# Scoring both softmax maps of a differential pair in one pass A unit, and one exponential for both maps in pass B

## What is computed

```python
def diff_block(qp, q):
    s = jnp.einsum('bqhmd,bkhmd->bhmqk', q.astype(f32), kd) * SCALE
    bias = table[t5_bucket(kpos[None, :] - qp[:, None])]
    s = s + jnp.transpose(bias, (2, 0, 1))[None, :, None]
    mask = (kpos[None, :] // CHUNK) <= (qp[:, None] // CHUNK)
    s = jnp.where(mask, s, NEG_INF)
    p = jax.nn.softmax(s, axis=-1)
    a = p[:, :, 0] - lam * p[:, :, 1]
    return jnp.einsum('bhqk,bkhe->bqhe', a, vd)
```

## Time and profile before

| | before |
|---|---|
| median of 3 runs | 2607.59 us (2605.26 to 2613.81) |
| the profiled execution | 2605.0 us |
| its span | 2603.2 us |
| PE busy | 2478.4 us (95%), 13569 instructions |
| DVE busy | 1374.3 us (53%), 2227 instructions |
| ACT busy | 942.9 us (36%), 1869 instructions |
| POOL busy | 386.0 us (15%), 398 instructions |
| granted TensorE clock, mean | 0.984 |

### The profile page before, as it was taken

One profiled execution on the slowest core, in us unless ns is written; L12 is line 12 of the kernel. 1 busy time (PEld: TensorE's weight loads), 2 busy tenths in 40 slices (PEclk: granted clock), 3 DMA queues, 4 the chain that ended last, 5 costly groups with the idle time before them and its releaser, 6 DMA issues.

```text
span 2603.2 us, 35097 instructions
## 1 busy us (share of the span) xinstructions
PE 2478.4 (95%) x13569; PEld 1977.2 (76%) x13569; DVE 1374.3 (53%) x2227; ACT 942.9 (36%) x1869; POOL 386.0 (15%) x398
## 2 busy tenths in 40 slices
PE   7999999999999999999988899899899989999998
PEld 5788888789999999999855565565565556888897
DVE  5311123315443333542368888788788786655553
ACT  4123331112222222111136645654664666322221
POOL 0100001121100000112352113103212242000000
PEclk9999999999999999999989999999999999999999
DMA  5688888958987666888560523235054023544432
GB/s 153 161 223 207 202 210 206 209 138 243 244 237 226 207 215 181 233 206 175 145 158 9 126 50 89 55 77 130 5 131 107 28 83 108 181 133 130 143 118 89
DMA packets 583892, 388.65 MB, mean 149 GB/s; under 512 B 318672, under 2 KB 538776, under 8 KB 577416
## 3 DMA queue, kind: packets, MB, share of 16 engines
q1 hardware_dynamic: 574592, 367.80, 53.8%
q0 software_dynamic: 9136, 18.63, 2.1%
HBM read 284.83 MB, written 134.79 MB: 161 GB/s over the span
## 4 chain that ended last, share of the span: by engine, by line
PE 75%; DVE 6%; SPq 5%; ACT 5%; issue 4%; DMA 3%; POOL 1%; DVEq 0%; ACTq 0%; POOLq 0%
PE p_acc L876 13%; PE p_acc L881 12%; PE p_acc L880 12%; PE a_op L2111 5%; PE a_sb L2086 4%; PE a_sb L2087 3%; PE a_op L2108 3%; PE a_sa L2064 2%; PE a_sa L2067 2%; PE e_U L1428 2%; PE e_U L1430 2%; PE e_U L1429 2%; ACT a_e L1924 2%; DVE a_nmax L1955 2%; PE a_sa L2065 2%
## 5 line engine op out<-in xcount | busy, mean ns | idle before, releaser
L876 PE MATMUL p_acc<-p_h_hi,p_w_hi 128*128 128x384 f32 (+1 forms) x1960 | 716.1, 365 | 11.9 <-DVE p_ev L586 5.5
L881 PE MATMUL p_acc<-p_h_hi,p_w_lo 128*128 128x384 f32 (+1 forms) x1920 | 688.0, 358 | 0.0
L880 PE MATMUL p_acc<-p_h_lo,p_w_hi 128*128 128x384 f32 (+1 forms) x1920 | 687.8, 358 | 0.0
L1955 DVE TENSOR_REDUCE a_nmax<-a_sa 128x1 f32<-128x1024 f32 (+7 forms) x384 | 347.2, 911 | 125.0 <-PE a_sa L2069 45.1
L1924 ACT ACTIVATE a_e<-a_sb 128x512 f32<-128x512 f32 (+3 forms) x640 | 310.4, 533 | 278.5 <-PE a_sb L2087 183.8
L876 PEld LDWEIGHTS p_acc<-p_h_hi,p_w_hi 128*128 128x128 f32 x1960 | 370.8, 189 | 52.7 <-issue 12.8
L881 PEld LDWEIGHTS p_acc<-p_h_hi,p_w_lo 128*128 128x128 f32 x1920 | 362.1, 189 | 30.4
L880 PEld LDWEIGHTS p_acc<-p_h_lo,p_w_hi 128*128 128x128 f32 x1920 | 362.6, 189 | 29.0
L692 DVE TENSOR_TENSOR p_w_lo<-p_raw,p_w_hi 128x1024 fp32r<-128x1024 f32 x96 | 125.6, 1308 | 368.8 <-ACT p_w_hi L619 368.7
L2086 PE MATMUL a_sb<-a_q,a_k 128*128 128x512 f32 (+2 forms) x640 | 276.5, 436 | 20.6 <-ACT a_e L1924 18.1
L2087 PE MATMUL a_sb<-a_q,a_k 68*128 68x512 f32 (+2 forms) x640 | 237.1, 374 | 0.0
(11 more groups left out here) (233 smaller groups left out, 3475.6 us busy)
## 6 DMA issues: line engine op xcount, KB each, us to landing
p_raw<-in_w_in SPq DMA_DIRECT2D x98, 512.0 KB, 5.7
s_k_raw<-scratch_kS SPq DMA_DIRECT2D x64, 512.0 KB, 6.9
scratch_kS<-in_cache_fox_k SPq DMA_DIRECT2D x32, 512.0 KB, 6.6
scratch_kS<-in_cache_diff_k SPq DMA_DIRECT2D x32, 512.0 KB, 6.4
s_v_raw<-in_cache_fox_v SPq DMA_DIRECT2D x8, 2048.0 KB, 11.0
s_v_raw<-in_cache_diff_v SPq DMA_DIRECT2D x8, 2048.0 KB, 10.0
a_q<-scratch_q_hi SPq DMA_DIRECT2D x32, 512.0 KB, 13.3
a_k<-scratch_k_hi SPq DMA_DIRECT2D x32, 512.0 KB, 15.2
```

The source lines that it names most:

```text
L876: nc.tensor.matmul(acc[a % 2][:, 0:n], hi, h_hi[p][:, k, at:at + n], start=(k == 0), stop=False)
L880: nc.tensor.matmul(acc[a % 2][:, 0:n], hi, h_lo[p][:, k, at:at + n], start=False, stop=False)
L881: last = nc.tensor.matmul(acc[a % 2][:, 0:n], lo, h_hi[p][:, k, at:at + n], start=False, stop=(k == DK - 1))
L1955: nc.vector.tensor_reduce(nmax[:, b % 2, c, col:col + 1], scores_of(ev[1]), axes, ALU.max, negate=True).then_inc(a_maxed, 1)
```

## The change

1. Pass A of a differential pair has units of both maps, `(b, None, t, c)`, with chunks of 512 keys. Map m takes bank m of the PSUM tile. PE does the two 128-row products, one per map, and then the two high-times-high products with 64 rows each, map 0 in array rows 0 to 63 and map 1 in rows 64 to 127. For this, `q2` and `k2` of map 1 hold their values in partitions 64 to 127 and the constants in the rows below. There are 160 such units instead of 192.
2. DVE adds one band for both maps (L1952 before) and takes both maxima in one instruction (L1955 before). ACT still makes one exponential per map, since each has its own bias; each now has up to 512 columns.
3. In pass B the two banks are one tile `sb`. One band addition (76 instead of 152 instructions) and one exponential (320 instead of 640) serve both maps. `b_scored` and `e_made` count units, not maps, so PE waits for the whole exponential of unit u before it writes either map of unit u+1.
4. `nmax`, `total` and `gap` hold up to 4 chunks, and the few small instructions that combine chunks do so for all of them at once.

```diff
-        sb_ = [s.ps(f"sb{m}", [P, QUERIES]) for m in range(MAPS)]
+        sb_ = s.ps("sb", [P, MAPS, QUERIES])
...
         for t in range(4):
+            if b // BLOCKS % 2:
+                A_UNITS += [(b, None, t, c) for c in range(Q + 1)]
+                continue
...
+    chunk = lambda b: CHUNK_KEYS // 2 if is_diff(b) else CHUNK_KEYS
+    a_cols = lambda a: a_width(a) * (2 if is_diff(a[0]) else 1)
...
-    a_work = list(itertools.accumulate([0] + [a_width(unit) + STEP for unit in A_UNITS]))
+    a_work = list(itertools.accumulate([0] + [a_cols(unit) + STEP for unit in A_UNITS]))
...
+    def maps_of(a):
+        return sa[a % 2][:].rearrange("p (m n) -> p m n", m=MAPS)
...
             elif ev[0] == "X" and is_diff(A_UNITS[ev[1]][0]):
...
-                nc.scalar.activation(scores_of(ev[1]), scores_of(ev[1]), ACT.Exp, bias=nmax[:, b % 2, c, col:col + 1],
-                                     accum_out=total[:, b % 2, c, col:col + 1]).then_inc(a_summed, 1)
+                for m in range(MAPS):
+                    col, own = 4 * m + t, maps_of(ev[1])[:, m, 0:a_width(A_UNITS[ev[1]])]
+                    last = nc.scalar.activation(own, own, ACT.Exp, bias=nmax[:, b % 2, c, col:col + 1],
+                                                accum_out=total[:, b % 2, c, col:col + 1])
+                last.then_inc(a_summed, 1)
...
             elif ev[0] == "E":
...
-                    nc.scalar.activation(e[:, u % E_SLOTS, m, cols], sb_[m][:, cols], ACT.Exp).then_inc(e_made, 1)
+                nc.scalar.activation(e[:, u % E_SLOTS, :, cols], sb_[:, :, cols], ACT.Exp).then_inc(e_made, 1)
...
-                for m in range(MAPS):
-                    dve.wait_ge(b_scored, 2 * u + m + 1)
-                    nc.vector.tensor_tensor(sb_[m][:, lo:hi], sb_[m][:, lo:hi], band[:, 1, lo - t0 * P:hi - t0 * P],
-                                            ALU.add).then_inc(b_biased, 1)
+                dve.wait_ge(b_scored, u + 1)
+                bias = band[:, 1:2, lo - t0 * P:hi - t0 * P].to_broadcast([P, MAPS, hi - lo])
+                nc.vector.tensor_tensor(sb_[:, :, lo:hi], sb_[:, :, lo:hi], bias, ALU.add).then_inc(b_biased, 1)
...
         def scores_a(a):
+            if is_diff(b):
+                wide = max(a_width(A_UNITS[a]), 2 * P)
+                ks = slice(c * chunk(b), c * chunk(b) + wide)
+                for m in range(MAPS):
+                    nc.tensor.matmul(maps_of(a)[:, m, 0:wide], q1[z][m][:, qs], k1[z][m][:, ks], start=True, stop=False)
+                for m in range(MAPS):
+                    rows = slice(m * HD, m * HD + HD)
+                    last = nc.tensor.matmul(maps_of(a)[:, m, 0:wide], q2[z][m][rows, qs], k2[z][m][rows, ks], start=False, stop=True)
+                last.then_inc(a_scored, 1)
+                return
...
         def scores_b(u):
+            if u:
+                pe.wait_ge(e_made, u)
             for m in range(MAPS):
-                if u:
-                    pe.wait_ge(e_made, 2 * u + m - 1)
```

More of the change, by code:

```diff
@@ L1576, in banded @@
         tile = 4 * (b % BLOCKS) + t
-        first = max((tile - 1) * P, c * CHUNK_KEYS)
-        end = c * CHUNK_KEYS + a_width(a)
+        first = max((tile - 1) * P, c * chunk(b))
+        end = c * chunk(b) + a_width(a)
         return (end - first, first - (tile - 1) * P) if is_diff(b) and first < end else None
@@ L1748, in load_map @@
             rows = slice(m * HD, (m + 1) * HD)
+            high = lo if z and m else hi
             tensor, part, x = ((q1, hi, "q_hi"), (k1, hi, "k_lo"), (q1, lo, "q_lo"), (k1, lo, "k_hi"),
-                               (q2, hi, "q_hi"), (k2, hi, "k_hi"))[n]
+                               (q2, high, "q_hi"), (k2, high, "k_hi"))[n]
             sp.dma_start(tensor[z][m][part, :].bitcast(F32), d[x][pair_of(f), rows, :]).then_inc(maps_in[z][m], 16)
@@ L1896, in scalar @@
                     act.wait_ge(f_dve, dve_at[b, "gap"])
-                    nc.scalar.activation(gap[:], gap[:], ACT.Exp).then_inc(f_act, 1)
+                    now = gap[:, 0:n_chunks(b), :]
+                    nc.scalar.activation(now, now, ACT.Exp).then_inc(f_act, 1)
                 elif ev[2] == 1:
@@ L2041, in scores_a @@
             if (b % BLOCKS, t, c) == (0, 0, 0):
-                pe.wait_ge(maps_in[z][m], 96 * (f // 2 + 1))
-                if m == 0:
+                for m_ in range(MAPS) if is_diff(b) else [m]:
+                    pe.wait_ge(maps_in[z][m_], 96 * (f // 2 + 1))
+                if not m:
                     pe.wait_ge(side_in[z], side_total(f))
@@ L2059, in scores_a @@
                     at = kt * P - k0
-                    if not is_diff(b) and kt == tile and 0 <= at < n_b:
+                    if kt == tile and 0 <= at < n_b:
                         adds.append((slice(at, at + P), causal[:, 0]))
                 high = (q2[z][m][0:ROW_C, qs], k2[z][m][0:ROW_C, k0:k0 + wide])
-                if is_diff(b):
-                    nc.tensor.matmul(out, q1[z][m][:, qs], k1[z][m][:, k0:k0 + wide], start=True, stop=False)
-                    last = nc.tensor.matmul(out, *high, start=False, stop=True)
-                else:
-                    last = nc.tensor.matmul(out, *high, start=True, stop=not adds)
-                    for cols, msk in adds:
-                        last = nc.tensor.matmul(out[:, cols], ident16[:], msk, start=False, stop=True)
+                last = nc.tensor.matmul(out, *high, start=True, stop=not adds)
+                for cols, msk in adds:
+                    last = nc.tensor.matmul(out[:, cols], ident16[:], msk, start=False, stop=True)
             last.then_inc(a_scored, 1)
@@ L2080, in scores_b @@
             ks = slice(kt * P, (kt + 1) * P)
+            if u:
+                pe.wait_ge(e_made, u)
             for m in range(MAPS):
-                if u:
-                    pe.wait_ge(e_made, 2 * u + m - 1)
-                out = sb_[m][:, c0:QUERIES]
+                out = sb_[:, m, c0:QUERIES]
                 qs = slice(Q * QUERIES + c0, (Q + 1) * QUERIES)
                 nc.tensor.matmul(out, k1[z][m][:, ks], q1[z][m][:, qs], start=True, stop=False)
-                nc.tensor.matmul(out, k2[z][m][0:ROW_C + 2, ks], q2[z][m][0:ROW_C + 2, qs], start=False,
-                                 stop=True).then_inc(b_scored, 1)
+                rows = slice(0, P if z and m else ROW_C + 2)
+                last = nc.tensor.matmul(out, k2[z][m][rows, ks], q2[z][m][rows, qs], start=False, stop=True)
+            last.then_inc(b_scored, 1)
         def product(u):
```

88 lines of the change are left out of this document (49 added, 39 removed).

## The result

| | before | changed |
|---|---|---|
| median | 2609.5 us (4 runs, 2605.3 to 2613.8) | 2692.2 us (4 runs, 2691.2 to 2700.9) |
| ratio, 95% interval | | 1.0324 [1.0306, 1.0343] |
| profiled execution, span | 2605.0, 2603.2 us | 2691.9, 2690.2 us |
| attention, first to last product of pass B | 882.4 us | 966.9 us |
| granted clock, mean of the span | 0.984 | 0.979 |

The account below looks back on a forecast made before the run. PE, busy 95% of the span, and what PE waits for were taken as the bound. Terms 21.6 - 18 + 73 = +77 us on the profiled 2605.0 gave 2682, as median 2684; range 2620 to 2735.

Parts of the forecast that it names:

- Pass B's one exponential: Pass B: PE waits for the merged exponential before the next unit; 83 us lost, 73 us after the deduction.
- The need of 1.39 us: Pass B, full unit without band: time from the end of its columns until PE may begin the next unit, 0.46 before.
- The walk: Pass B: waits added over all 319 intervals between units, need against PE's work between; 93.4 us against 10.2 before.
- four groups with fox pass A or none: Pass B intervals, fox beside fox and differential without differential pass A: waits 22.8, 7.8, 14.3 and 23.5 us.
- four places with nothing between: Pass B: 4 intervals where PE has no work between two units; 5.5 us of waits.
- "10 us" taken off: Pass B: deduction from the 83 us, for new waits that only replace PE's waits for DVE.
- The columns and the switch: Pass A: paired row halves save 30.9 us of columns; entering and leaving 64 rows loses 52.5 us.
- pass A's PE time grows by 21.6 us: Pass A: net of columns saved and switches to 64 rows and back, counted whole as 21.6 us lost.
- Pass A's waits: Pass A: fewer PE stalls for ACT's exponential, with longer exponentials counted against it; 18 us gained.
- 1.1 us times 28 intervals: Pass A: intervals with two units fall from 44 to 16, each saving a stall of about 1.1 us.
- the free switch with hidden waits: Rival: 64-row switch costs nothing and pass B's waits hide; 2583 us, deciding under 0.19 us a unit; chance 0.08.
- ACT: Rival: ACT becomes the bound in differential pass A, half to all of 47 us on top; 2708 to 2731, chance 0.14.

Follow-up runs that it names:

- e1: Kernel before with pass B's change alone (one exponential and one band addition for both maps), pass A as before: 2691.9 us, ratio 1.032.
- e4: Kernel before with 64 instead of 66 array rows in pass A's 320 second products of differential pairs, all else unchanged: 2751.7 us, ratio 1.0521.
- e3: e2 with pass A's high products kept at 66 rows from partition 0, so no row halves: 2602.0 us, ratio 0.9979.
- e2: Kernel before with pass A's change alone (units of both maps, 64-row products), pass B per map as before: 2608.2 us, ratio 1.000.
- e11: Changed kernel with pass A's high products at 66 rows from partition 0, no row halves: 2701.2 us, ratio 1.0364.
- e8: Kernel before with one exponential for both maps in the 80 fox units that have value products behind them: 2608.5 us, ratio 1.0013.
- e9: Kernel before with one exponential for both maps in the other 80 fox units, with no value product behind them: 2648.1 us, ratio 1.0161.
- the best version: e3 with STEP (fixed columns a pass A unit counts for in the order) 0 instead of 300: 2588.4 us, ratio 0.9933.

## Why the prediction was right, and where its terms were off

**Pass B's one exponential** was the right place and mechanism. The need of 1.39 us is met to the hundredth at 1593.22. The walk's four groups with fox pass A or none come to 63 us above before, and its four places with nothing between to some 5 more, before anything was taken off; 61.9 were measured in those stretches. What was mis-sized is the "10 us" taken off. By the rest, e1 loses 63 of the 93 us of the walk (102.8 against 10.2 for its order), so 30 did not show (by the same idea as in pass A, waits that took the place of others; no run shows which), and the clock takes 23, which no term of mine had. The two errors cancel: that the forecast of 2684 came within 8 us of 2692 is in that part luck.

**The columns and the switch** (30.9 gained, 52.5 lost): both prices hold, 0.235 us for the pair and 0.19 an end. The Trainium skill says in "TensorEngine Tiling (Array Packing)", Key Properties, that changing the tiling mode drains TensorE; the runs agree and put the price to it. The Trainium skill's span model ("TensorE: Matmul & The Clock Gate", Measured speedup vs the span model), one matmul and about 4 ns for each further tile, agrees with the trace inside the pair, whose two records start and end 3 ns apart. It has no term for getting there and back between products of 128 rows, and here that costs 380 ns a visit. The prediction's working for it calls the 32-bit product two-pass; no run shows passes, only the 0.42 us that 512 such columns take in rows 5, and e4 measured the price without it. But the term "pass A's PE time grows by 21.6 us" was put on the path whole. Of it 6 us showed with 300 as STEP, 3 with 0.

**Pass A's waits** (18 us gained): e3 has only this and 2 us of padding, and it gained 4 us, by the rest none. The step that failed is 1.1 us times 28 intervals as a gain on the path. PE's own idle ahead of pass A fell only from 41.2 to 35.4 us in e3: the double intervals were thinned out, but, as far as this goes, units of both maps hold the tile longer (two exponentials and two reads), and PE waited for it elsewhere; where was not traced. The 118.2 us of rows 8, which the prediction reads as the weight load's, are 76.9 of the weight load and 41.2 of the product. +21.6 - 18 = +3.6 was right by sum (e2: +2), with both members several times too large; that too is luck. They are two sides of the same idle, and should not have been added as if independent.

One number of the rivals does not come out of its own terms: the free switch with hidden waits turns at (30.9 + 18 - 25) / 160 = 0.15 us a unit, not 0.19. Nothing else rests on it.

**ACT** stays beside PE: e1 and e11, without and with its longer pass A and both without halves, have the same rest within 1 us. The 9 us between their times are clock.

**The clock** was missing from the sum altogether. 15 us of the 83 are that, taken against the 23 runs of before. In the changed kernel, five windows of 10 us and then PE in the fourth of them:

```profile
1610.00:1620.00 10.00, 8.89 (x30) 3.25 (x29) 6.60 (x6) 3.07 (x3) 5.33 (x3) 0.83 0.08 32
1620.00:1630.00 10.00, 9.79 (x45) 5.09 (x45) 8.71 (x13) 6.21 (x16) 2.53 (x5) 1.00 0.02 3
1630.00:1640.00 10.00, 8.31 (x41) 4.21 (x37) 8.52 (x14) 7.06 (x20) 2.33 (x6) 1.00 0.00 1
1640.00:1650.00 10.00, 9.57 (x32) 5.16 (x32) 3.75 (x5) 5.83 (x16) 0.94 (x2) 0.66 0.01 1
1650.00:1660.00 10.00, 8.69 (x36) 4.05 (x36) 8.85 (x12) 8.11 (x20) 5.47 (x4) 1.00 0.07 26
```

```profile
1640.42 0.73 PE L2082 MATMUL a_sa<-a_k,a_q 128*128 128x512 f32 x2 [1.90 <-ACT a_sa L1910]
1641.09 0.78 PE L2085 MATMUL a_sa<-a_k,a_q 64*128 64x512 f32 x2
...
1642.39 0.63 PE L2120 MATMUL a_sb<-a_q,a_k 68*128 68x512 f32 x1
1642.82 0.63 PE L2118 MATMUL a_sb<-a_q,a_k 128*128 128x512 f32 x1
1643.24 0.63 PE L2120 MATMUL a_sb<-a_q,a_k 68*128 68x512 f32 x1
...
1648.71 0.40 PE L2118 MATMUL a_sb<-a_q,a_k 128*128 128x512 f32 x1
1648.94 0.40 PE L2120 MATMUL a_sb<-a_q,a_k 68*128 68x512 f32 x1
```

PE waits 1.90 us, then works for some 7 us at the lower level, 1.2 GHz: 512 columns take 0.43 us instead of 0.23, and the window's mean is 0.66. From 1340 us of the span to the end of the attention the profile of the changed kernel has 15 such stretches, 68 us in all, and that of before has 9, 44 us (one of them behind 1.87 us of idle that ends at 1661.41). Shortly ahead of each of the 15 PE had paused for 1.2 to 2.1 us. There the changed kernel has 28 pauses of 1.2 us or more, the kernel before 15. So the lower clock goes with the pauses in these two kernels, but not each pause brings it, three of the 9 came behind pauses of 0.8 us alone, and in e4, with its many switches, the first and longest stretch (20 us) has no pause over 0.6 us ahead of it. What brings the clock down is therefore left open.

## What to carry to other kernels

A merged instruction on a double-buffered chain moves its start to the last producer and its release to its own end. Count, for each place, the work that the waiting engine has in between (here 0.46 us against a need of 1.39), and merge only where it covers: e8 did so for nothing, e9 paid 42 us for the same 80 instructions. And do not add work removed and waits removed on one engine: where it idles for another anyway, 20 us of work more or less moved the time by 3 to 6 (and by 10 in the merged kernel, where the clock took it back and more).

## What the runs showed that was not expected

- A visit to 64-row products costs 0.38 us of PE time between products of 128 rows (0.19 at each end, 320 visits in e4), while 66 rows cost nothing (start to start 0.24).
- The granted clock is a term of its own: 44 us missing in the kernel before, 32 in the best version, 59 to 76 in the three with all of pass B merged, 112 in the one that switches most. With it two executions of one kernel can lie up to 38 us apart (e4: 2716.3 at 0.972, 2754.6 at 0.954).
